# The root of a layer's first norm moved from the rows to what is computed from them, in a two-layer hybrid encoder step

## What is computed

```python
n = rms_norm(x, ln1_w)                      # x * rsqrt(mean(x*x) + eps) * w, one root for each token
proj = n @ w_in                             # 1024 -> 7 * 512
q, k, v, g, gate_b, gate_c, hc = split(proj)
qf, kf = rope(q, pos), rope(k, pos) * HD**-0.5
o, r_new = retention_chunkwise(qf, kf, v, r0, chunk)     # 4 heads of 128
ret_out = silu(g) * group_norm(o) * ret_norm_w
u = gate_c * hc
conv_out = gate_b * causal_conv3(u)         # new_buf: the last rows of u
x = x + concat([ret_out, conv_out]) @ w_out
x = x + square(relu(rms_norm(x, ln2_w) @ w_up)) @ w_down
```

## Time and profile before

| | |
|---|---|
| median of 3 runs | 1367.63 us (1367.59 to 1367.64) |
| the profiled execution: time, span | 1367.56 us, 1364.9 us |
| PE, DVE, ACT, POOL busy in the span | 97%, 80%, 46%, 13% |
| mean granted TensorE clock | 0.988 |

### The profile page before, as it was taken

The page is one execution under the profiler, slowest core; times in us unless marked ns, Lnnn a source line. Parts: engine busy times, 40 slices in busy tenths (PEclk is TensorE's granted clock), DMA queues, the critical chain, the costliest instruction groups (busy, mean ns, idle before and its releaser), DMA issues.

```text
span 1364.9 us, 21348 instructions
## 1 busy us (share of the span) xinstructions
PE 1327.6 (97%) x8804; PEld 1283.3 (94%) x8804; DVE 1095.7 (80%) x1283; ACT 632.7 (46%) x734; POOL 181.2 (13%) x161
## 2 busy tenths in 40 slices
PE   6899999999999999999999999999999999999995
PEld 5789999999999999999978899999999999999995
DVE  5736878999968958958986477899998697696797
ACT  4313645466436435435532254455653454443552
POOL 1632110011000000000125211011100000000002
PEclk8899999999999999999999999999999999999998
DMA  8345565646544635537234746655554634644532
GB/s 259 93 123 156 123 164 141 139 124 155 124 124 124 154 94 143 138 96 206 37 94 130 214 97 145 164 125 139 115 148 124 148 103 126 177 90 130 155 62 77
DMA packets 117863, 180.20 MB, mean 132 GB/s; under 512 B 4804, under 2 KB 43844, under 8 KB 117768
## 3 DMA queue, kind: packets, MB, share of 16 engines
q1 hardware_dynamic: 85528, 123.91, 27.8%
q0 software_dynamic: 31680, 54.53, 24.2%
q10 hardware_dynamic: 560, 0.41, 0.1%
HBM read 171.42 MB, written 7.41 MB: 131 GB/s over the span
## 4 chain that ended last, share of the span: by engine, by line
PE 81%; DVE 15%; issue 2%; POOL 1%; ACT 1%; DVEq 0%; POOLq 0%; ACTq 0%
PE pair L920 37%; PE pair L1003 28%; PE pair L757 11%; DVE ring L1897 3%; DVE x L1858 1%; DVE a_ring L2042 1%; PE pair L799 1%; DVE acc L1713 1%; DVE xn L1736 1%; DVE s_raw L2077 1%; POOL root_of L1541 1%; PE pair L819 1%; DVE raws L1907 1%; PE pair L823 1%; DVE mlp_in_lo L2077 1%
## 5 line engine op out<-in xcount | busy, mean ns | idle before, releaser
L1003 PE MATMUL pair<-a_ring,ring 128*128 128x320 f32 x3360 | 496.0, 309 | 0.0
L1003 PEld LDWEIGHTS pair<-a_ring,ring 128*128 128x128 f32 x3360 | 493.5, 188 | 0.6
L1177 ACT ACTIVATE ring<-raws 128x1024 fp32r<-128x1024 f32 x304 | 315.7, 1055 | 307.6 <-PE pair L1003 130.8
L920 PE MATMUL pair<-mlp_in_hi,ring 128*128 128x320 f32 x1792 | 397.3, 309 | 4.8 <-DVE ring L1897 2.8
L1897 DVE TENSOR_TENSOR ring<-raws,ring 128x1024 fp32r<-128x1024 f32 x304 | 367.2, 1223 | 42.3 <-ACT ring L1177 41.6
L920 PEld LDWEIGHTS pair<-mlp_in_hi,ring 128*128 128x128 f32 x1792 | 300.2, 188 | 6.0 <-issue 3.3
L920 PE MATMUL pair<-mlp_in_lo,ring 128*128 128x320 f32 x896 | 276.7, 309 | 0.0
L920 PEld LDWEIGHTS pair<-mlp_in_lo,ring 128*128 128x128 f32 x896 | 168.2, 188 | 0.2
L1858 DVE TENSOR_TENSOR x<-x,pair 128x640 f32<-128x640 f32 x140 | 115.0, 821 | 40.0 <-PE pair L1003 39.8
L757 PE MATMUL pair<-pair_a,norm_hi 128*128 128x512 f32 x320 | 106.0, 414 | 10.0 <-DVE pair_a L1690 5.4
L920 PE MATMUL pair<-ch_in_hi,ring 128*128 128x320 f32 x512 | 113.6, 309 | 1.2 <-issue 1.2
(11 more groups left out here) (180 smaller groups left out, 1421.4 us busy)
## 6 DMA issues: line engine op xcount, KB each, us to landing
raws<-in_w_mlp_up SPq DMA_DIRECT2D x32, 1024.0 KB, 5.5
raws<-in_w_mlp_down SPq DMA_DIRECT2D x32, 1024.0 KB, 5.5
raws<-in_w_in SPq DMA_DIRECT2D x16, 1024.0 KB, 6.5
raws<-in_w_mlp_up POOLq DMA_DIRECT2D x16, 1024.0 KB, 8.5
raws<-in_w_mlp_down POOLq DMA_DIRECT2D x16, 1024.0 KB, 9.0
w_raw<-in_w_in SPq DMA_DIRECT2D x11, 1024.0 KB, 5.2
past_state<-in_state_ret SPq DMA_DIRECT2D x16, 512.0 KB, 7.1
raws<-in_w_in POOLq DMA_DIRECT2D x8, 1024.0 KB, 9.7
```

What stands on the lines that cost most here:

```text
L920: mm = pe.matmul(out[:, n, 0:HALF], item_half(item, h, a)[:, k, n * P:(n + 1) * P], tokens[c][:, k], start=(i in (B11, B21, SUM_1112) and ...
L1003: mm = pe.matmul(out[:, n, 0:HALF], item_half(item, h, a)[:, k, n * P:(n + 1) * P], a_item[:, c, k], start=(i in (B11, B21, SUM_1112) and ...
L1177: nc.scalar.activation(item_half(item, h, 0), raw_half(quad, RAW_OF[i], h), ACT.Copy).then_inc(half_hi.sem, 1)
```

## The change

K, V, Q and the gates read weighted x in place of the normed rows, and the root is applied behind the product:

- `rows_hi` and `rows_lo` read x and the weight directly, two instructions for each pair of k-tiles in place of one (xn and `normalise` go);
- `cols_of` copies the root into a column for each token tile (four copies of 32 partitions each for a slice), and `rope` and `copy_v` multiply by that column;
- the root's square, spread over the partitions, multiplies C's first half (`scale_c`) and H's second half (`scale_h`, two instructions); the root, spread, multiplies G (`scale_g`, four) and the convolved rows (`scale_z`, two). These, `square_roots`, `spread_squares` and `spread_roots` are new on DVE in each layer;
- layer 0's slices become 128, 256 and 256 tokens, the second half of the first weights comes in four pieces ahead of the second slice of x, and PE's sums of squares move behind K's second group (group 2 and on); the roots of layer 0 are taken inside the K stage;
- in layer 1 the sum of the second half's squares moves from the head of group 1 to the middle of group 2;
- ACT's and DVE's written orders are new in all stages.

```diff
-SLICES = (((0, P), (P, HALF), (HALF, TOK)), ((0, HALF), (HALF, TOK)))
+SLICES = (((0, P), (P, 3 * P), (3 * P, TOK)), ((0, HALF), (HALF, TOK)))
...
                     def rows_there(k, first=(n == STAGE_START[chunk]), chunk=chunk):
-                        if (layer, n, k) in ((0, 0, 4), (0, 1, 7)):
-                            sum_first(n + 1)
-                        elif layer and (n, k) == (1, 0):
+                        if layer == 0 and (n, k) in ((2, 0), (2, 7), (3, 7)):
+                            sum_first(n - 2 + k // 7)
+                        elif layer and (n, k) == (2, 4):
                             sum_rows("n1", layer, 1)
...
             def rows_hi(layer, s, pair):
                 first, last = SLICES[layer][s]
-                act.wait_ge(xn_ready, rows_to(layer, s, pair))
-                nc.scalar.activation(norm_hi[:, 2 * pair:2 * pair + 2, first:last], xn[:, pair, :, 0:last - first], ACT.Copy
-                                     ).then_inc(n1_hi, 1)
+                if layer == 0:
+                    act.wait_ge(x_in[s][pair // 2], 16)
+                else:
+                    i = ((B21, B22), (SUM_ALL, SUM_1222))[s][pair // 2]
+                    act.wait_ge(x_added.sem, x_added.at(layer - 1, x_adds_to(NBLK - 1, i, pair % 2)))
+                for k in (2 * pair, 2 * pair + 1):
+                    ins = nc.scalar.activation(norm_hi[:, k, first:last], x[:, k, first:last], ACT.Copy,
+                                               scale=norm_weights[:, 2 * layer, k:k + 1])
+                ins.then_inc(n1_hi, 1)
...
+            def cols_of(layer, s):
+                first, last = SLICES[layer][s]
+                dve.wait_ge(root_ready, norm_of("n1", layer, s) + 1)
...
+                for g in range(4):
+                    js = range(g + (first // 32 - g + 3) // 4 * 4, last // 32, 4)
+                    rows = slice(32 * g, 32 * (g + 1))
+                    ins = nc.vector.tensor_copy(root_cols[rows, js[0] // 4:js[-1] // 4 + 1], root_of[rows, js[0]:js[-1] + 1:4])
+                ins.then_inc(cols_ready, 1)
...
-                nc.vector.tensor_tensor(dst.rearrange("p (h f) -> p h f", f=HD // 2), src, tab[0], ALU.mult)
+                dve.wait_ge(cols_ready, cols_to(layer, slices_of(layer, p)[-1]))
+                root = root_cols[:, p:p + 1]
+                nc.vector.scalar_tensor_tensor(out=dst.rearrange("p (h f) -> p h f", f=HD // 2), in0=src, scalar=root,
+                                               in1=tab[0], op0=ALU.mult, op1=ALU.mult)
...
+                def scale_g(half, h):
+                    dve.wait_ge(root_spread, spread_of("n1", layer) + 1)
+                    dve.wait_ge(hidden_summed.sem, hidden_summed.at(layer, c_sums_to(OUT, (B22, SUM_1222)[half], h)))
+                    g = halves((t12, t11)[half], h)
+                    nc.vector.tensor_tensor(g, g, spread(half, 2), ALU.mult).then_inc(g_scaled.sem, 1)
...
                 for p in range(NT):
                     rope(layer, "K", p, k_rot[:, ORDER[p]], k_rotated)
+                    if (layer, p) == (0, 0):
+                        mean_first(1)
+                        add_first_squares(2)
+                        cols_of(0, 1)
+                    elif (layer, p) == (0, 1):
+                        mean_first(2)
+                    elif (layer, p) == (0, 2):
+                        cols_of(0, 2)
                     if p in (2, 3):
                         split_unit(layer, 1, p - 2)
```

More of the change, by code:

```diff
@@ L79 @@
 NORM = {x: n for n, x in enumerate(NORMS)}
+SPREADS = [(kind, layer, t) for layer in range(DEPTH) for kind, t in (("n1", 0), ("n2", 0), ("n2", 1))] + [("end", t) for t in range(2)]
+SPREAD = {x: n for n, x in enumerate(SPREADS)}
 ROW_PAIRS = KT // 2
@@ L569, in norm_of, with spread_of @@
             return NORM[(kind, t) if kind == "end" else (kind, layer, t)]
+        def spread_of(kind, layer, t=0):
+            return SPREAD[(kind, t) if kind == "end" else (kind, layer, t)]
         def squares_at(kind, layer):
@@ L723, in sum_first @@
                 width = SLICES[0][s][1] - SLICES[0][s][0]
[L724 to L735, removed]
+                pe.wait_ge(first_added, 3 * (s + 1))
+                if s == 2:
+                    pe.wait_ge(sums_turned, 1)
+                pe.matmul(sum_bank[s % 2][:, 0:width], ones[:], first_squares[s][:, 0], start=True, stop=True
+                          ).then_inc(sums_ready, 1)
             def sum_rows(kind, layer, t):
@@ L856, in small @@
                 mm.then_inc(small_done.sem, 1)
-            sum_first(0)
             for layer in range(DEPTH):
@@ L1136, in _ @@
             for dh in range(2):
-                first_square(2, dh)
+                first_square(0, dh)
+            for dh in range(2):
+                first_square(1, dh)
             for two in range(ROW_PAIRS):
                 rows_hi(0, 2, two)
+            for dh in range(2):
+                first_square(2, dh)
             for layer in range(DEPTH):
@@ L1224, in gate_of @@
                     src = halves((t12, t11)[half], h)
-                    act.wait_ge(hidden_summed.sem, hidden_summed.at(layer, c_sums_to(OUT, (B22, SUM_1222)[half], h)))
+                    act.wait_ge(g_scaled.sem, g_scaled.at(layer, 2 * half + h + 1))
                     if half == 0:
@@ L1488, in _ @@
                 gate_of(0, 0)
+                copy_product(OUT, SUM_111222, 1)
                 weight_half(13, 1)
@@ L1588, in _ @@
             pool.wait_ge(norm_weights_in, 16)
-            for s, (first, last) in enumerate(SLICES[0]):
-                root_rows(s, last - first)
             for layer in range(DEPTH):
@@ L1597, in _ @@
                 for p in range(NT):
+                    if layer == 0 and p < len(SLICES[0]):
+                        root_rows(p, *SLICES[0][p])
                     rotate(layer, "K", p, k_rot[:, ORDER[p]], k_rotated)
@@ L1738, in scale_rows @@
                     in1=mean_root[:, first:last], op0=ALU.mult, op1=ALU.mult)
-            def normalise(layer, s, pair):
-                first, last = SLICES[layer][s]
-                dve.wait_ge(root_spread, NORM["n1", layer, s] + 1)
-                for i in range(2):
-                    ins = scale_rows(xn[:, pair, i, 0:last - first], layer, 2 * pair + i, first, last)
-                ins.then_inc(xn_ready, 1)
             def rows_lo(layer, s, pair):
                 first, last = SLICES[layer][s]
-                ks = slice(2 * pair, 2 * pair + 2)
                 dve.wait_ge(n1_hi, rows_to(layer, s, pair))
-                nc.vector.tensor_tensor(norm_lo[:, ks, first:last], xn[:, pair, :, 0:last - first],
-                                        f(norm_hi[:, ks, first:last]), ALU.subtract).then_inc(n1_lo, 1)
+                for k in (2 * pair, 2 * pair + 1):
+                    ins = nc.vector.scalar_tensor_tensor(
+                        out=norm_lo[:, k, first:last], in0=x[:, k, first:last], scalar=norm_weights[:, 2 * layer, k:k + 1],
+                        in1=f(norm_hi[:, k, first:last]), op0=ALU.mult, op1=ALU.subtract)
+                ins.then_inc(n1_lo, 1)
             def finish_rows(t, pair):
-                dve.wait_ge(root_spread, NORM["end", t] + 1)
+                dve.wait_ge(root_spread, spread_of("end", DEPTH, t) + 1)
                 for k in (2 * pair, 2 * pair + 1):
@@ L2369, in _ @@
                 hidden_sum(OUT, B22, 0)
+                scale_g(0, 0)
                 weight_half(13, 0)
```

506 lines of the change are left out of this document (267 added, 239 removed).

## The result

The changed kernel takes **1392.36 us** (median; 1391.36 to 1396.06), the kernel before 1367.64 on the same chip: ratio 1.0186, 95% interval 1.0167 to 1.0204. It is 25 us slower, where 1355.0 was forecast and the range ended at 1359.5. The profiled execution took 1392.26 us, its span is 1390.4.

What follows compares the result with a forecast made beforehand. PE, busy 97% of the span, was taken to bound the kernel, with DVE setting the pace from 219 to 320 us of each layer. 1367.56 - 13.2 - 2.4 + 1.5 + 1.6 = 1355.1, said as 1355.0 us; range 1350.5 to 1359.5.

Steps and rivals of the forecast that it cites:

- The start of layer 0: Up to Q's first group in layer 0: Q starts at 55.8 in place of 69.04, 13.2 us gained, bounds 11 to 15.
- The switch of layers: From layer 0's end into layer 1's K: new waits of 1.6 and 2 us, still 2.4 gained, bounds 0.5 and 4.
- the rival on the clock: New waits of 1.5, 1.6 and 2 us bring PE's clock down, switch gain gone: 1358.4 to 1360 us; chance 0.12.
- The turns in CH: In CH, PE waits 0.7 us a layer for the last tile's `norm_heads`, 1.5 in all, bounds 0 and 2.5.
- The scaling work: DVE's 10.4 us of added products a layer cost PE 0.8 a layer, 1.6 in all, bounds 0 and 5.8.
- The cover for the 7.5 us: Ahead of 219 us in each layer, DVE's 10.1 us idle for ring halves hides 7.5 us of scaling, costed at nothing.
- The step that failed: In `up(0)`, PE's starts after its two earlier waits come only 0.7 and 0.4 to 1.5 us later.
- The slower one: DVE is behind before 219 us, all 10.4 us land on the full stretch in both layers: 1369.3 us; chance 0.05.
- slower (0.04): Outcome for the whole kernel: slower than the kernel before, beyond 0.2% or 2.7 us; chance 0.04.

Runs made afterwards that it cites:

- f4: e1 with three moves: V's last copy earlier on ACT, third chunk's split and V's first copy earlier on ACT, layer 1's first rope before second root's columns: 1358.18 us.
- f3: e1 without the multiplications of C, H, G and the convolved rows by the root, semaphores kept: 1361.36 us.
- g3: f4 without the multiplications of C, H, G and the convolved rows by the root: 1354.90 us.
- e1: Changed kernel with the order of ACT and DVE inside up and down products put back as before the change: 1364.68 us.
- h1: Changed kernel with one move on POOL: first up product's adding DMA for SUM_1222 ahead of making the second root: 1375.02 us.
- g4: e2 plus one move on POOL: first up product's adding DMA for SUM_1222 ahead of making the second root: 1366.16 us.
- h2: Changed kernel in its own orders with e2's swap, f2's moves, hidden sums earlier in first up product, f4's three moves and g4's POOL move: 1355.59 us.
- h4: Kernel before the change with the POOL move alone, adding DMA for SUM_1222 ahead of the second root: 1367.67 us.
- e3: Changed kernel with B22's second hidden sum on DVE ahead of item 6's first weight half and the root's spreading, every up product: 1393.13 us.
- f2: e2 plus, in first up product, B11's second-half copy ahead of ACT's waiting weight half and second root's mean one weight half earlier on DVE: 1368.29 us.
- e2: Changed kernel with one ACT swap in the first up product: first input difference's upper part ahead of the waiting weight half: 1384.30 us.

## Why the prediction was wrong

- **The start of layer 0: right within 1 us.** First matmul at 7.81 (8.6 forecast), a wait of 1.33 for the sum in group 2 (1.5), 0.67 for `rope`'s bank (0.8), 2.1 in V's first (1.4), one of 0.7 in group 4 not forecast; Q at 56.89 (55.8), so 12.2 us gained (13.2). The start differs from trace to trace by more than that: Q stands at 56.1 to 58.9 in the kernels with this start, at 69.0 to 69.9 in the three with the old one.
- **The switch of layers: wrong by 3 us.** The wait for low rows was 1.3 (1.6 forecast), that for `rope` 3.1 (2), and behind it the mean clock was 0.57 of full speed from 714 to 718: 1.6 us, the rival on the clock. Nothing was gained. Of the 1.1 us by which the wait for `rope` was too long, 0.7 are the four root copies, which took 1.41 at this place and not the 0.7 of the sum. The ropes of K's first two groups needed only the first root, and I took their place behind the second as given; f4 moved them.
- **The turns in CH: wrong place.** `norm_heads` cost 0.2 us a layer, not 0.7. But V's last copy stood behind another `norm_heads` and cost 1.6, and the low parts of V's spread rows and of K came 1.1 late. I had gone through DVE's order here, and not ACT's.
- **The scaling work: nearly right, at another place.** 1.15 us a layer with the old order of `up` and `down` (f3, g3), where the sum has 0.8, within its bounds. It falls in `down(OUT)` and ahead of the first wait of `up(0)`; that wait and the next are 1.00 and 1.39 with the scaling and without. The cover for the 7.5 us held: ahead of `down(OUT)` e1 and f3 take the same time from Q (171.15 and 171.19).
- **The step that failed** is the end of that paragraph: "So PE starts at 302.59 + 0.7 and at 319.16 + 0.4 to 1.5". It looked at the two waits that PE had before and asked what DVE's moved instructions do to them. Both stayed small. But the change had moved instructions on three in-order queues here, and two of the moves put work that PE needs behind an instruction that waits for memory: `in_diff_hi_of(0)` behind a weight half on ACT (8.9 us in all by h1 against g4), and, through later means on DVE, POOL's DMA behind its root (17.3 us by h1). That is 26 of the 37 us between forecast and result. The 10.6 us from g4 to h2 are the rest: f4's three moves and the small waits for the sums. Of each layer's 18.7 us 4.2 are the clock behind the two stalls. This step is not the whole miss: e1, in which both waits are as before, is at 1364.68, 9.7 us over the forecast and outside its range, mostly by the switch, V's copy and the low parts.
- **The rivals.** The slower one had the right sign and the wrong mechanism: DVE was not behind, it stood idle for 6.1 and 6.2 us, where before it had been busy 99.28 of 101 us and 20.81 of the next 21. The one on the clock held in part, with waits of a size that it didn't consider; its sum is also wrong, since two or three times 1.7 us and the gain at the switch gone make 1360.8 to 1362.5, not 1358.4 to 1360. The chance for slower (0.04) was too small: the order of `up(0)` was followed on DVE only, and nothing in the rows excluded a wait that comes from another queue.

## What to carry to other kernels

When a change moves instructions, go through every in-order queue, and at each instruction that waits for memory write down what now stands behind it that it needn't; the price is up to the whole wait, not the length of what was moved. The DMA that a queue issues is such an instruction too: POOL's adding DMA waited for a root that it doesn't use, with no cost before (h4) and 17 us after. And read which instruction of the releaser's line ended last, not the line alone: e3 moved a sum of the right line and the wrong product.

## What the runs showed of the hardware

An adding DMA of 1 MB took longer the sooner a plain load of 1 MB was issued behind it. In the changed kernel the one for SUM_ALL was issued at 317.52 and the load at 318.47: it landed after 12.2 us, and the load took 11.6. In h1 it was issued at 312.83 and the load at 317.67: 8.6 us, and 7.6 for the load. With the load 2.3 us behind (f2) it took 9.4; with the load 4.4 us behind, in the kernel before, 8.4. So an issue 4.7 us earlier was a landing 8.3 us earlier. Loads issued later, with no adding DMA under way, took 5.1 in both. No run moved the load alone, so that it is the load which draws the adding DMA out is argued from these rows, not shown.

The clock behind a wait of 3.1 us fell in one trace and not in another. Windows of e1 and then of f3, around the end of this wait:

```profile
699.00:703.00 4.00, 3.44 (x8) 0.57 0.00 0
```

```profile
699.00:703.00 4.00, 4.00 (x18) 1.00 0.00 0
```

That was worth 1.6 us (72 matmuls in 18.18 us against 16.62), in a place where both kernels do the same work. Ten traces have this wait of 3.1 us: the 72 matmuls took 16.62 in f3, 18.05 to 18.24 in seven, and 19.45 and 19.52 in e2 and h1. What decides between these is not shown. The Trainium skill, "TensorE: Matmul & The Clock Gate", section "HAM oscillation", says that waits between bursts bring the array back to the low clock: the rows agree for the waits of 7.35 and 6.33; for the one of 3.1 they agree in nine traces of ten.

A product of 128x20 on DVE took 1.87 us beside POOL. The timelines of DVE and POOL in the kernel after:

```profile
56.98 1.87 DVE L1772 TENSOR_TENSOR root_squared<-root_of 128x20 f32<-128x20 f32 x1
```

```profile
55.00 3.83 POOL L1591 TENSOR_TENSOR v_spread<-v,const 128x1024 f32<-128x1024 f32 x1 [3.70 <-ACT v L1174]
```

It ends at 58.85, POOL's at 58.83, as if it stood until POOL was done; no trace has this product without POOL beside it. The Trainium skill, "Trainium Architecture — The Big Picture", section "What this means for kernel authors", says that DVE and GpSimd contend for a port pair by an exclusive lock; this pair of rows agrees. The four root copies, for which the prediction took 0.7 us, took 0.61 to 0.68 where POOL was idle, and 1.41 and 1.75 beside POOL's work:

```profile
26.76 0.61 DVE L1767 COPY root_cols<-root_of 32x1 f32<-32x1 f32 x4
...
692.16 0.68 DVE L1767 COPY root_cols<-root_of 32x3 f32<-32x3 f32 x4 [0.48 <-POOL root_of L1559]
...
711.50 1.41 DVE L1767 COPY root_cols<-root_of 32x2 f32<-32x2 f32 x4 [2.17 <-POOL root_of L1559]
```

The first two agree with the long end, which the prediction took by the Trainium skill, "VectorE: DVE Perf Modes", section "Two Vector instructions with no wait between them". Not settled is what the scaling costs in the changed kernel's own order of `up` and `down`, since f3 and g3 have the old one, and which of its products costs it: no run left out one alone.
